# A second home for one 2 MB weight load, and fp32 token gathers of which two move into the first expert

## The chip, the cores and the metric

One Trainium2 chip, one core of it. The metric is device time of one execution in microseconds (us). Engines: TensorE (PE) multiplies, VectorE (DVE) and ScalarE (ACT) do elementwise work, GpSimd (POOL) here only splits weights, and SyncE (SP) issues nearly all loads from memory.

## What is computed

Two transformer blocks on 256 tokens of 1024 features, all in fp32. The first has attention and retention heads, then a mixture of 32 experts of which each token takes four, then a gated side product. The second has attention, a state-space branch and a dense FFN. What matters here is the mixture:

```python
logits = (xt @ w_router + b_router).astype(jnp.float32)
top_vals, top_idx = lax.top_k(logits, TOP_K)
gates = jax.nn.softmax(top_vals, axis=-1)
...
def expert_block(args):
    xb, e = args
    hgu = xb @ w_up_gate[e] + b_up_gate[e]
    x_glu = jnp.minimum(hgu[:, :D_EXPERT], SWIGLU_LIMIT)
    x_lin = jnp.clip(hgu[:, D_EXPERT:], -SWIGLU_LIMIT, SWIGLU_LIMIT)
    hact = x_glu * jax.nn.sigmoid(SWIGLU_ALPHA * x_glu) * (x_lin + 1.0)
    return hact @ w_down[e] + b_down[e]
...
return jnp.zeros((t, d), xt.dtype).at[slot_tok].add(ys * slot_gate[:, None].astype(xt.dtype))
```

`w_up_gate[e]` is 1024 x 2048 and `w_down[e]` 1024 x 1024 in fp32: 12 MB for each expert, 384 MB in all.

## The kernel before, in words

Everything lives in two tensors on the chip. `ring` has 12 slots of 128 x 2048 fp32 (1 MB each); `arena` holds activations and scratch, and its areas are reused from stage to stage. Outside the experts a weight piece lands in one of slots 0 to 7, ScalarE writes its rounded copy (`w_high`, type fp32r) into one of slots 8 to 11 (L1272), GpSimd replaces the piece by the rest (`w_low`, L2311), and TensorE makes three fp32r products of the parts (`product`, L524 to L526).

The experts use the weights unsplit, in fp32. One expert is six loads of 2 MB, each into two neighbouring slots: four of up weights (`UPS = 4`) and two of down weights, at slots `EXPERT_SLOT = (4, 6, 8, 10, 0, 2)`. TensorE counts the semaphore `w_used` up by one for each weight piece or expert load that it has finished with; SP waits for that count before it overwrites a home. SP's program is in order: the split pieces, then `first_expert(j)` in the order `FIRST_EXPERT = (0, 1, 2, 4, 3, 5)`, the first two of them early, then `expert_loads(e, e)` for experts 1 to 31 (L447 to L473). `before_experts` is 20, the number of split pieces ahead of the experts. Behind the experts come the next stage's pieces, first four of `w_ple_gate`.

Each expert computes at most 64 tokens (`CAP`). Tokens are gathered for a group of four experts at once: a **gather round** (`gather_round(q)`, L852) multiplies the token matrix (128 x 128 stationary pieces) by a one-hot matrix `OH4` of 256 columns (4 experts x 64 places) for two of the eight feature chunks. The tokens are the normalised state in two fp32r parts, `XNH` and `XNL`: ScalarE writes the high part (L1399), VectorE the rest (`token_low`, L1867). So a round is 2 chunks x 2 token blocks x 2 parts = 8 matmuls. VectorE scales each round's result from PSUM into the group's token buffer (`group_round_out`, L1930), `XG[0]` or `XG[1]` in turn.

Ahead of the loop TensorE makes all four rounds for the first group, into PSUM banks 6, 4, 5, 7, with three bias matmuls (L921) behind the first. The loop (L926) is written out for eight experts. For one expert: bias matmuls (`up_bias`, L873) with the selector `SEL` that VectorE prepares (L1926, L1927, semaphore `sel`), 8 chunks x 4 up matmuls (L883), the scatter of the expert before (L908), the spread of the gate matrix (L867), transposes of the hidden values (L890), 16 down matmuls (L901), and one gather round for the next group (L852). `q` is the expert's place in its group of four. A plain fp32 matmul stands in the trace as two records of one instruction each; an fp32r matmul as one.

Between the router and the loop VectorE's order is `token_low(0)`, top four, mask, `token_low(1)`, gates, slot numbers (L1901 to L1904), one-hot matrices (L1920), the four round results with `select(0)` behind the second, the overflow flags, and two multiplications that write the whole normalised state into `XN` in fp32 (L1951), which only a pass for experts with over 64 tokens reads.

## Time and profile before

| what | us |
|---|---|
| three runs | 1588.88, 1590.39, 1590.72 |
| median | 1590.39 |
| span of the profiled execution, first to last instruction | 1586.7 |
| TensorE busy | 1465.7 (92% of the span) |
| VectorE, ScalarE, GpSimd busy | 477.8, 412.1, 459.6 |
| bytes moved | 502.30 MB, 317 GB/s over the span |
| experts' up matmuls (L883), busy | 460.2 |
| experts' down matmuls (L901), busy | 235.3 |

The profiled execution's own device time is not listed apart from its span; the span lies 2.2 to 4.0 us below the three runs. A busy share is an average over stages with different limits: the experts' stage takes from about 175 to 1106 us of the span, and the split products fill the rest. The granted TensorE clock is 0.988 of full speed in the mean.

### The profile page before, as it was taken

The page shows a single profiled execution, that of the slowest core. Times are in us where ns is not written, and L with a number is a line of the kernel's source. Part 1 is how long each engine was busy: PE and PEld are TensorE (multiplying, and loading weights), DVE is VectorE, ACT ScalarE, POOL GpSimd, SP SyncE. Part 2 cuts the span into 40 slices and gives each one's busy share as a digit, 9 for nine tenths or more (in the row PEclk, how much of TensorE's full clock was granted, in tenths as well). Part 3 has the DMA queues.
Part 4 walks back from the last instruction along what each step waited for, and adds up shares of the span by engine and source line. Part 5 has one row for each costly group of instructions (what it writes and reads, how often), then busy time and mean ns, then how long its engine had stood idle before and what let it go on. Part 6 is the DMA issues. An engine that isn't in the chain of part 4 may idle for free.

```text
span 1586.7 us, 18714 instructions
## 1 busy us (share of the span) xinstructions
PE 1465.7 (92%) x7556; PEld 832.7 (52%) x7557; DVE 477.8 (30%) x844; ACT 412.1 (26%) x521; POOL 459.6 (29%) x356
## 2 busy tenths in 40 slices
PE   8999999998898889999888999899899999999998
PEld 7877533333333333333333333333698776799986
DVE  6536411111111111111111111112467586333211
ACT  6354301001001011010010010011754834453332
POOL 6836000000000000000000000001687763779994
PEclk9999999999999999999999999999999999999999
DMA  9533899999999999999999999999564332545540
GB/s 346 200 118 97 364 428 428 428 428 427 426 428 428 427 427 427 427 427 427 428 428 427 427 427 429 427 428 400 164 211 162 107 106 79 194 152 186 186 159 27
DMA packets 91174, 502.30 MB, mean 317 GB/s; under 512 B 7836, under 2 KB 38164, under 8 KB 66388
## 3 DMA queue, kind: packets, MB, share of 16 engines
q1 hardware_dynamic: 89600, 498.71, 77.6%
q10 hardware_dynamic: 1491, 2.36, 0.5%
q8 instruction: 68, 1.11, 0.3%
q14 instruction: 15, 0.12, 0.0%
HBM read 500.00 MB, written 1.05 MB: 316 GB/s over the span
## 4 chain that ended last, share of the span: by engine, by line
PE 54%; DMA 34%; DVE 5%; ACT 3%; issue 2%; POOL 2%; SPq 0%; DVEq 0%; ACTq 0%
DMA ring<-in_w_up_gate 32%; PE PS L883 15%; PE PS L524 9%; PE PS L526 9%; PE PS L525 9%; PE PS L901 5%; POOL w_low L2311 2%; DMA ring<-in_w_ple_gate 1%; PE PS L852 1%; PE PS L1148 1%; ACT w_high L1272 1%; PE PS L890 1%; DVE arena L1969 0%; DVE arena L1966 0%; DVE arena L1964 0%
## 5 line engine op out<-in xcount | busy, mean ns | idle before, releaser
L2311 POOL TENSOR_TENSOR w_low<-ring,w_high 128x512 fp32r<-128x512 f32 (+1 forms) x352 | 459.4, 1341 | 1105.9 <-ACT w_high L1272 1105.4
L883 PE MATMUL PS<-ring,arena 128*64 128x512 f32 x2048 | 460.2, 602 | 31.0 <-DMA ring<-in_w_up_gate 31.0
L883 PEld LDWEIGHTS PS<-ring,arena 128*64 128x64 f32 x2048 | 142.9, 138 | 332.1 <-issue 272.4
L901 PE MATMUL PS<-ring,arena 128*64 128x512 f32 x1024 | 235.3, 614 | 28.2 <-ACT arena L1428 28.2
L1419 ACT ACTIVATE arena<-arena 128x512 f32<-128x512 f32 x32 | 20.1, 630 | 765.8 <-DVE arena L1963 765.8
L1272 ACT ACTIVATE w_high<-ring 128x2048 fp32r<-128x2048 f32 (+1 forms) x89 | 166.5, 1881 | 124.0 <-PE PS L526 101.0
L1963 DVE TENSOR_SCALAR arena<-PS 128x512 f32<-128x512 f32 x32 | 22.1, 691 | 466.6 <-PE PS L883 466.6
L901 PEld LDWEIGHTS PS<-ring,arena 128*64 128x64 f32 x1024 | 75.2, 140 | 166.2 <-issue 166.2
L524 PE MATMUL PS<-w_high,XNT_h 128*128 128x512 f32 (+1 forms) x336 | 135.5, 403 | 5.9 <-DVE XNT_l L1676 4.6
L524 PE MATMUL PS<-XNT_h,w_high 128*128 128x256 f32 (+1 forms) x464 | 130.8, 282 | 2.2 <-DVE XNT_l L1659 1.3
L526 PE MATMUL PS<-w_high,XNT_l 128*128 128x512 f32 (+1 forms) x336 | 131.5, 391 | 0.0
L525 PE MATMUL PS<-w_low,XNT_h 128*128 128x512 f32 (+1 forms) x336 | 131.4, 391 | 0.0
L525 PE MATMUL PS<-XNT_l,w_high 128*128 128x256 f32 (+1 forms) x464 | 130.3, 281 | 0.0
L526 PE MATMUL PS<-XNT_h,w_low 128*128 128x256 f32 (+1 forms) x464 | 130.3, 281 | 0.0
L1972 DVE COPY arena<-PS 128x512 f32<-128x512 f32 x32 | 22.1, 691 | 282.6 <-PE PS L901 282.6
L524 PEld LDWEIGHTS PS<-XNT_h,w_high 128*128 128x128 f32 (+1 forms) x464 | 86.1, 186 | 3.5 <-issue 1.8
L525 PEld LDWEIGHTS PS<-XNT_l,w_high 128*128 128x128 f32 (+1 forms) x464 | 86.2, 186 | 0.2
L526 PEld LDWEIGHTS PS<-XNT_h,w_low 128*128 128x128 f32 (+1 forms) x464 | 86.2, 186 | 0.1
L524 PEld LDWEIGHTS PS<-w_high,XNT_h 128*128 128x128 f32 x336 | 63.5, 189 | 24.1 <-issue 8.4
L525 PEld LDWEIGHTS PS<-w_low,XNT_h 128*128 128x128 f32 x336 | 63.6, 189 | 14.3 <-issue 1.0
L526 PEld LDWEIGHTS PS<-w_high,XNT_l 128*128 128x128 f32 x336 | 63.3, 188 | 14.7
L908 PE MATMUL PS<-arena 64*128 64x512 f32 x256 | 63.6, 615 | 0.0
(369 smaller groups left out, 1429.1 us busy)
## 6 DMA issues: line engine op xcount, KB each, us to landing
ring<-in_w_up_gate SPq DMA_DIRECT2D x128, 2048.0 KB, 23.8
ring<-in_w_down SPq DMA_DIRECT2D x64, 2048.0 KB, 22.2
ring<-in_w_in SPq DMA_DIRECT2D x35, 1024.0 KB, 5.3
ring<-in_w_gate_up SPq DMA_DIRECT2D x22, 1024.0 KB, 5.1
ring<-in_w_down SPq DMA_DIRECT2D x11, 1024.0 KB, 4.7
ring<-in_w_out SPq DMA_DIRECT2D x8, 1024.0 KB, 4.9
ring<-in_w_ple_gate SPq DMA_DIRECT2D x4, 1024.0 KB, 22.2
ring<-in_w_ssd_proj SPq DMA_DIRECT2D x4, 1024.0 KB, 4.9
```

The lines of the kernel that those rows point to most:

```text
L524: nc.tensor.matmul(out, lhs[0], rhs[0], start=start, stop=False)
L525: nc.tensor.matmul(out, lhs[0], rhs[1], start=False, stop=False)
L526: return nc.tensor.matmul(out, lhs[1], rhs[0], start=False, stop=stop)
L852: ins = nc.tensor.matmul(PS[:, bank, (c % 2) * 256:(c % 2) * 256 + 256], part[:, tb * D + c * P:tb * D + (c + 1) * P], OH4[:, tb * 256:(tb ...
L883: ins = nc.tensor.matmul(PS[64 * (n % 2):64 * (n % 2) + 64, 4 + n // 2, :], x, w[:, n * 512:(n + 1) * 512], start=False, stop=c == KC - 1, ...
L901: ins = nc.tensor.matmul(PS[64 * n:64 * n + 64, 7, :], lhs, w[:, k, n * 512:(n + 1) * 512], start=(j, k) == (0, 0), stop=(j, k) == (1, 3))
L908: ins = nc.tensor.matmul(PS[:, 2 * tb + n, :], SPT[64 * n:64 * n + 64, tb * P:(tb + 1) * P], YS[64 * n:64 * n + 64, :], start=False, stop= ...
L1272: nc.scalar.activation(HIGH[m % BUF][:, 0:size(key)], slot(raw_slot(key))[:, 0:size(key)], ACT.Copy).then_inc(sem("w_high"), 1)
L1419: nc.scalar.activation(SIG, GLU, ACT.Sigmoid, scale=1.702).then_inc(sem(sig_out), 1)
L1963: ts(GLU, PS[:, 4, :], 7.0, None, ALU.min).then_inc(sem("glu"), 1)
L1972: V.tensor_copy(YS, PS[:, 7, :]).then_inc(sem("y_slots"), 1)
L2311: ins = nc.gpsimd.tensor_tensor(LOW[raw_slot(key)][:, at], slot(raw_slot(key))[:, at], HIGH[m % BUF][:, at].bitcast(F32), ALU.subtract)
```

## The change

It does five things.

1. The gathers read the normalised state in plain fp32. ScalarE's activation (the former L1399) writes it straight into `XN`, in the order of features that the experts' loads have. `XNH`, `XNL`, `token_low` and VectorE's two multiplications go. A round is now 2 chunks x 2 token blocks = 4 fp32 matmuls, with `OH4` in fp32.
2. The 2 MB of the arena that held `XNH` and `XNL` become `ODD_UP`, the home of the first up load of each odd expert, with a semaphore of its own, `landed_odd`. Even experts keep slots 4 and 5.
3. Expert 1's first up load is issued as soon as the last `w_out` piece is used, behind two of expert 0's. For later experts `first_up` waits for the use of the first up load two experts back.
4. Only rounds 0 and 1 of the first group are made ahead of the loop (banks 6 and 7). Rounds 2 and 3 of each group are made inside its first expert, in front of its third and fifth up chunk. Rounds 0 and 1 of the next group are made behind the second and third expert of a group; the first and fourth have none behind them.
5. VectorE builds the next group's one-hot matrices in the group's second expert instead of its first.

The core of the diff:

```diff
-        XNH, XNL = pair("XNS", 8192, 10240, 2048)
+        ODD_UP = area(8192, 4096)
-        OH4 = parts_at("OH4", arena_byte + 4 * 18688, 2 * GROUP * CAP)
+        OH4 = area(18688, 2 * GROUP * CAP)
-        FIRST_ROUNDS = (6, 4, 5, 7)
+        FIRST_ROUNDS = (6, 7)
...
-                sp.dma_start(slots2(EXPERT_SLOT[j]), src).then_inc(landed[EXPERT_SLOT[j]], 16)
+                if odd and j == 0:
+                    sp.dma_start(ODD_UP, src).then_inc(landed_odd, 16)
+                else:
+                    sp.dma_start(slots2(EXPERT_SLOT[j]), src).then_inc(landed[EXPERT_SLOT[j]], 16)
...
+            def first_up(e, odd):
+
+                sp.wait_ge(sem("w_used"), e * PER_EXPERT + (before_experts - 2 * PER_EXPERT + 1))
+                expert_load(e, 0, odd)
...
-            for j in FIRST_EXPERT[2:]:
+            for j in FIRST_EXPERT[2:4]:
                 first_expert(j)
-            with sp.Fori(1, E) as e:
-                expert_loads(e, e)
+            sp.wait_ge(sem("w_used"), place[("out", 1, 1)] + 1)
+            expert_load(1, 0, odd=True)
+            for j in FIRST_EXPERT[4:]:
+                first_expert(j)
+            with sp.Fori(0, E // 2 - 1) as i:
+                expert_loads(i * 2 + 1, i * 2 + 1, 1)
+                first_up(i * 2 + 2, odd=False)
+                expert_loads(i * 2 + 2, i * 2 + 2, 1)
+                first_up(i * 2 + 3, odd=True)
+            expert_loads(E - 1, E - 1, 1)
...
-                        for part in (XNH, XNL):
-                            ins = nc.tensor.matmul(PS[:, bank, (c % 2) * 256:(c % 2) * 256 + 256], part[:, tb * D + c * P:tb * D + (c + 1) * P],
-                                                   OH4[:, tb * 256:(tb + 1) * 256],
-                                                   start=(tb, part is XNH) == (0, True), stop=(tb, part is XNL) == (1, True))
+                        ins = nc.tensor.matmul(PS[:, bank, (c % 2) * 256:(c % 2) * 256 + 256], XN[:, tb * D + c * P:tb * D + (c + 1) * P],
+                                               OH4[:, tb * 256:(tb + 1) * 256], start=tb == 0, stop=tb == 1)
...
                     if q == 0:
-                        pe.wait_ge(sem("x_slots"), e + 3)
+                        pe.wait_ge(sem("x_slots"), e + 2)
                     up_bias()
                     for c in range(KC):
+                        if q == 0 and c == 2:
+                            gather_round(2)
+                        if q == 0 and c == 4:
+                            pe.wait_ge(sem("x_slots"), e + 3)
+                            gather_round(3)
                         if q == 0 and c == 6:
                             pe.wait_ge(sem("x_slots"), e + 4)
...
                     down(e)
-                    if q == 0:
+                    if q == 1:
                         pe.wait_ge(sem("onehot"), i * 2 + (u // GROUP + 2))
-                    gather_round(q)
+                    if q in (1, 2):
+                        gather_round(q - 1)
...
-                nc.scalar.activation(feature_pairs(XNH, tb), pairs_of(X, tb), ACT.Copy, scale=stat[:, 6 + tb:7 + tb]).then_inc(sem("xn_high"), 1)
+                nc.scalar.activation(feature_pairs(XN, tb), pairs_of(X, tb), ACT.Copy, scale=stat[:, 6 + tb:7 + tb]).then_inc(sem("tokens"), 1)
...
-            token_low(0)
...
-            token_low(1)
...
-            for tb in range(NTB):
-                link(ts(XN[:, tb * D:(tb + 1) * D], X[:, tb * D:(tb + 1) * D], stat[:, 6 + tb:7 + tb], None, ALU.mult))
```

The order of SP's instructions where the experts' loads begin, before: two loads of expert 0 (up, down), two more, then the loop over experts with the six loads of one each. The words in brackets are the semaphores that an instruction waits for.

```order
L448 DMA ring<-in_w_up_gate 128x4096 [waits w_used]
L448 DMA ring<-in_w_down 128x4096 [waits w_used]
L448 DMA ring<-in_w_up_gate 128x4096 [waits w_used]
L448 DMA ring<-in_w_down 128x4096 [waits w_used]
L472 UNCONDITIONAL_BRANCH
L472 ISA
L448 ISA [waits w_used]
L448 DMA ring<-in_w_up_gate 128x4096
```

The same place now:

```order
L456 DMA ring<-in_w_up_gate 128x4096 [waits w_used]
L456 DMA ring<-in_w_down 128x4096 [waits w_used]
L454 DMA arena<-in_w_up_gate 128x4096 [waits w_used]
L456 DMA ring<-in_w_up_gate 128x4096 [waits w_used]
L456 DMA ring<-in_w_down 128x4096 [waits w_used]
L489 UNCONDITIONAL_BRANCH
L489 ISA
L456 ISA [waits w_used]
L456 DMA ring<-in_w_up_gate 128x4096
```

Expert 1's first up load (to `arena`) now stands ahead of the last two loads of expert 0, and the loop begins with expert 1's second up load.

TensorE's order from the last gather matmuls ahead of the loop into expert 0, before (`OH_58` and `XNS` are `OH4` and the two token parts, `landed4` and `landed6` the arrival of the first two up loads):

```order
L852 MATMUL PS<-OH_58,XNS_h 128x256
L852 MATMUL PS<-OH_58,XNS_l 128x256
L925 UNCONDITIONAL_BRANCH [waits bias_low,late_in]
L925 ISA
L931 REGISTER_ALU [waits sel]
L873 MATMUL PS<-BUP,SEL 128x512 [waits x_slots]
L873 MATMUL PS<-BUP,SEL 128x512
L880 ISA
L883 MATMUL PS<-ring,arena 64x512 [waits landed4]
L883 MATMUL PS<-ring,arena 64x512 x7
L883 MATMUL PS<-ring,arena 64x512 [waits landed6]
```

The same place now:

```order
L945 UNCONDITIONAL_BRANCH [waits bias_low,late_in]
L945 ISA
L951 REGISTER_ALU [waits sel]
L891 MATMUL PS<-BUP,SEL 128x512 [waits x_slots]
L891 MATMUL PS<-BUP,SEL 128x512
L964 ISA
L903 MATMUL PS<-ring,arena 64x512 [waits landed4]
L903 MATMUL PS<-ring,arena 64x512 x7
L872 MATMUL PS<-arena 128x256 x4
L897 ISA
L903 MATMUL PS<-ring,arena 64x512 [waits landed6]
```

Round 2 (L872, four matmuls) has moved from ahead of the loop to between the first and the second up load of expert 0; round 3 stands likewise between the second and the third.

## Rows read from the trace of the kernel before

**Rows 1.** The page, part 2: GB/s in 40 equal slices of the span

```profile
GB/s 346 200 118 97 364 428 428 428 428 427 426 428 428 427 427 427 427 427 427 428 428 427 427 427 429 427 428 400 164 211 162 107 106 79 194 152 186 186 159 27
```

**Rows 2.** Windows, TensorE: length, busy time (instructions), granted clock, DMA share, GB/s

```profile
260.00:600.00 340.00, 306.69 (x1402) 0.98 1.01 428
```

**Rows 3.** The page, part 5: the experts' up matmuls

```profile
L883 PE MATMUL PS<-ring,arena 128*64 128x512 f32 x2048 | 460.2, 602 | 31.0 <-DMA ring<-in_w_up_gate 31.0
```

**Rows 4.** The chain of waits, end of the experts: start, us, what

```profile
1081.46 21.25 DMA ring<-in_w_ple_gate
...
1102.80 1.92 ACT w_high L1272
...
1104.79 19.98 POOL w_low L2311 x16
```

**Rows 5.** Timeline of SP's DMA issues: start, us, what, how many

```profile
154.06 0.34 SPq L448 DMA_DIRECT2D ring<-in_w_up_gate  x1
...
165.52 0.33 SPq L448 DMA_DIRECT2D ring<-in_w_up_gate  x1
...
179.72 0.35 SPq L448 DMA_DIRECT2D ring<-in_w_up_gate  x1
183.14 3.77 SPq L448 DMA_DIRECT2D ring<-in_w_up_gate  x2
...
198.21 3.77 SPq L448 DMA_DIRECT2D ring<-in_w_down  x2
206.85 3.77 SPq L448 DMA_DIRECT2D ring<-in_w_up_gate  x2
```

**Rows 6.** Windows of 2 us around the start of the experts

```profile
170.00:172.00 2.00, 2.00 (x8) 0.50 0.97 418
...
178.00:180.00 2.00, 2.00 (x12) 1.00 0.03 8
180.00:182.00 2.00, 2.00 (x12) 1.00 0.67 147
182.00:184.00 2.00, 2.00 (x12) 1.00 0.90 385
```

**Rows 7.** Timeline of VectorE ahead of the experts: start, us, what, [idle before <-releaser]

```profile
165.27 1.40 DVE L1867 SCALAR_TENSOR_TENSOR XNS_l<-arena,stat,XNS_h 128x512 fp32r<-128x512 f32 x2
...
167.44 0.22 DVE L1901 SCALAR_TENSOR_TENSOR slot_of<-PS,arena 128x64 f32<-128x64 f32 x1
...
173.45 0.69 DVE L1930 TENSOR_TENSOR arena<-PS,stat 128x512 f32<-128x512 f32 x1 [2.10 <-PE PS L852]
...
174.25 0.19 DVE L1927 CAST SEL<-cst 64x64 fp32r<-64x64 f32 x1
```

**Rows 8.** Timeline of TensorE ahead of the experts

```profile
166.39 0.39 PE L838 MATMUL PS<-arena,cst 128*128 128x32 f32 x2
...
167.58 0.64 PE L843 MATMUL PS<-cst,gate_of 128*32 128x128 f32 x8 [0.49 <-DVE gate_of L1898]
169.04 0.36 PE L852 MATMUL PS<-OH,XNS_h 128*128 128x256 f32 x1 [0.83 <-DVE OH L1920]
...
170.42 1.48 PE L921 MATMUL PS<-BUP,SEL 128*128 128x512 f32 x3
...
175.21 0.73 PE L873 MATMUL PS<-BUP,SEL 128*128 128x512 f32 x2
```

**Rows 9.** Timeline of TensorE: a gather round, and fp32 matmuls of 128x256

```profile
201.40 0.39 PE L852 MATMUL PS<-OH,XNS_h 128*128 128x256 f32 x1
...
202.46 0.63 PE L873 MATMUL PS<-BUP,SEL 128*128 128x512 f32 x2
...
1261.99 1.89 PE L1129 MATMUL PS<-arena 128*128 128x256 f32 x8
1263.72 1.02 PE L1138 MATMUL PS<-arena,cst 128*128 128x512 f32 x2
```

73 lines of the change are left out of this document (42 added, 31 removed).

## Prediction

> **What bounds the kernel now.** I read the page's slices first: from the sixth slice to the twenty-sixth the memory queues move 426 to 429 GB/s without a break [rows 1], and the windows show their share at 1.01 [rows 2]. That is the experts' loop: 192 transfers of 2048 KB, six for each of 32 experts (four of up weights, two of down weights). I call each a pair, since it fills two slots of the ring, and number them 1 to 192 in the order in which TensorE uses them. At 427 GB/s a pair of 2.097 MB takes 4.91 us. TensorE is idle before the up matmuls for 31.0 us in all because pairs are missing [rows 3], and the chain that ended last runs through the loop on DMA, leaves it over the first ple_gate piece, which comes behind pair 192 in the same queue, and goes on over the splits on GpSimd [rows 4]. So inside the loop nothing on TensorE, VectorE or ScalarE counts as long as the queue stays full. What counts is when the queue becomes full for good, and how much is left to move at that time.
>
> SP's issues show how it fills [rows 5]. Pairs 3 and 5 go out at 154.06 (two 2 MB loads one behind the other), pairs 4 and 6 at 165.52, and then all six pair homes are taken. Pair 7 waits until expert 0 has used pair 1: 179.72. Between, the queue is dry: 8 GB/s in 178 to 180, 147 and 385 in the next two windows [rows 6]. Those two hold 1.06 MB, which is 2.5 us at 427 GB/s, so full flow began at 181.5, 1.8 us after the issue. From there the queue is never dry: pair 11 would need 181.5 + 4 x 4.91 = 201.1, and the use of pair 5 that frees its home came at 198.21, with 1.8 us for the start 200.0. That margin of 1.1 us is small, and the prediction turns on it.
>
> **The change, part by part.**
>
> *The second home.* Pair 7 (the first of expert 1) is issued at 154.06 behind pairs 3 and 5. Five pairs then run from 155.8 to 155.8 + 5 x 4.91 = 180.4, with no gap. This fills the two dry stretches, moves 4.91 us of work ahead of the loop, and lets the queue wait for pair 2 instead of pair 1. Pairs 4 and 6 land some 5 us later than before; expert 0 needs pair 4 at about 190, so this costs nothing.
>
> *The order of work until expert 0.* The two `token_low` pieces go. The one of 1.40 us at 165.27 lay in front of the gates [rows 7]; without it VectorE waits for the position matmuls instead, which end at 166.39 + 0.39 = 166.78 [rows 8], not moved since TensorE comes to them from the side product. VectorE's slot arithmetic began at 167.44, so it gains 0.6 us, and the first gather round starts at 168.46 instead of 169.04. The two XN multiplications after the flags go too; nobody waited for them.
>
> *The price of a round.* A gather round was 8 fp32r matmuls, 1.06 us from 201.40 to 202.46 [rows 9]. It becomes 4 fp32 matmuls of 128x256, which stand in the trace as 8 records. The nearest rows are the 8 such records at 1261.99, followed at 1263.72 by the next line: 1.73 us, at full clock and behind full-width matmuls [rows 9]. The old round began with a first record 0.1 us longer, so bounds are 1.73 and 1.95; I take 1.85.
>
> *Start of expert 0.* Before, rounds 2 and 3 covered VectorE's copy and the selector; now TensorE waits for `sel`: 0.69 us for the copy and 0.99 us from the copy's start to the selector's end [rows 7]. With the clock at 2.4 GHz: 168.46 + 1.75 + 0.7 (three bias matmuls) + 1.75 = 172.7, drained at 172.8, plus 1.05 = 173.85 against 175.21 [rows 8]: 1.35 us earlier. But before, the granted clock was 0.50 from 170 to 172 [rows 6], that is 1.2 GHz, and the round from 169.04 to 170.42 and the three bias matmuls, 1.48 us with their drain, felt it. TensorE had been idle for 0.49 and 0.83 us and had run small matmuls before it fell. Now the first of these gaps goes and a new one of 1.05 us comes in front of expert 0. If the clock falls all the same, be it there or a little later, it costs 1.7 us, and expert 0 is 0.35 us later than before. Call the shift S: -1.35 to +0.35. One row with a fall after more idling does not decide it; I take the middle, -0.5.
>
> *Expert 0.* Two rounds of 1.85 us lie inside its up matmuls, in front of pairs 2 and 3. Nothing hides them: expert 0's pairs have landed, TensorE is never idle there. VectorE's copy of round 2 (0.69 us) is hidden by pair 2's 3.43 us. Now the queue: pair 8 can go at 183.14 + 1.85 + S, flowing at 186.8 + S. Pair 9 follows at 192.1 + S (it was issued at 186.58, the last 0.33 us of the 3.77 from 183.14), pair 10 behind it. Pair 11 needs expert 0's first down pair used: 198.21 + 3.7 + 1.8 + S = 203.7 + S. Pairs 8 to 10 are through at 201.9 + S or sooner, so the queue goes dry once more and **pair 11 sets the end**. Pair 12 has 1.5 us of margin (issued at 201.65 before; 201.65 + 3.7 + 1.8 = 207.1 against 208.6), pair 13 has a free home, and pair 14 is at 214.7 against 218.4, because expert 0 no longer ends with a round. From there on the queue is full.
>
> *Sum.* Before, pair 11 flowed at 201.1; now at 203.7 + S. All that comes behind it is the same in bytes and order, and the chain leaves the loop over the first ple_gate piece. So the end moves by 2.6 + S: +1.25 to +2.95, and with 1.73 or 1.95 for a round +1.0 to +3.2; I take **+2.1 us**. The extra home gives 4.9 us of work ahead; waiting for pair 2 and then for the down pair, behind two added rounds, takes it back and a little more.
>
> By the Trainium skill (DMA: Bandwidth & Descriptors, section "Anatomy of one DMA") a transfer costs about 2.0 us plus its bytes at 436 GB/s, which would be 4.8 us a pair. The rows say 427 GB/s and 1.8 us; with the page's figures pair 11 would have flowed at 200.9 before and 203.9 + S now, a loss 0.4 us greater.
>
> *What costs nothing.* The steady rounds: per expert 0.79 us more on TensorE, covered by the queue (29.5 us for six pairs against 27.13 us from 179.72 to 206.85 [rows 5]). The last round, which expert 31 no longer makes: 1.06 us off TensorE, but the chain behind the loop is held by ple_gate's landing at 1102.7 and 19.98 us of GpSimd splits [rows 4]. ple_gate issued earlier: it stands behind pair 192 as before.
>
> **The rivals.**
>
> *A. TensorE becomes the bound (slower).* 31 experts with 0.79 us more are 24.5 us, and TensorE's idle time on missing pairs is 31.0 us [rows 3]. That leaves 6.5 us. Against: fewer waits should mean fewer falls of the clock, each of which costs about 1.7 us. For: falls in the last experts come too late to be made up. It decides from about four falls more than before; with two beyond that the price is 3.4 us, so 1590.4 + 2.1 + 3.4 = 1596. Beside it: the Trainium skill (TensorE: Matmul & The Clock Gate, "HAM oscillation") has TensorE throttled when it idles for data again and again, so fewer waits would help it, and this rival would be less likely. Chance 0.13.
>
> *B. Only pair 8 binds.* If the stretch from expert 0's last up matmul to its down pair were shorter than 198.21 shows, or rounds cost no more than the old ones, the end moves by 186.8 + S - (181.5 + 4.91) = +0.4 + S, 1590.3 with the middle S. Against: the down stretch isn't touched. Chance 0.09.
>
> *C. The queue itself gets faster (faster).* With seven homes more loads are in the queue. The share is 1.01 and the mean 428 GB/s [rows 2], with slices up to 429 [rows 1]. If the mean rose by 0.7%, the 186 pairs behind pair 6 (913 us) would shrink by 6.4, giving 1590.4 + 2.1 - 6.4 = 1586. Against: the share shows no empty time to win. Chance 0.06.
>
> **How the numbers follow.** The sum stands against the profiled execution, whose span is 1586.7 us; its own time isn't listed apart, but the three runs (1588.88 to 1590.72) lie 2.2 to 4.0 us above the span, and the change touches nothing outside. I set it on the median: 1590.39 + 2.1 = **1592.5 us**. Forecast 0.72, A 0.13, B 0.09, C 0.06. A measurement of this kernel can tell about 0.2% (3.2 us) from no change. Of the forecast's 0.72 some 0.14 lie above +3.2 us, since two clock falls or the dear round are enough: slower 0.27, faster 0.06 (C), same 0.67. The range leaves out C and the far half of A: with the runs' own 0.9 us it is 1588.4 to 1596.5.
>
> **What would show it.** In the trace of the changed kernel: SP issues an up load to the arena right behind the two at 154; the next one only at about 184.5; expert 0's first down pair is used at about 201.4; GB/s drops between 202 and 203.5, a dip that is absent now; no dip from there on; TensorE's idle time on missing pairs falls from 31 to some 10 us; the first ple_gate split begins about 2 us after 1102.80. I am wrong if the queue is full from pair 8 on (B), if TensorE no longer waits for pairs in the last experts (A), or if expert 0 starts outside 173.8 to 175.6.

## The result and the profile after

| | before | changed |
|---|---|---|
| median of 20 runs, us | 1589.83 | 1592.22 |
| lowest to highest | 1587.31 to 1592.10 | 1590.17 to 1594.19 |
| span of the profiled execution | 1586.7 | 1588.8 (its own time 1590.65) |
| TensorE busy | 1465.7 | 1480.2 |
| TensorE idle for missing pairs, up matmuls | 31.0 | 19.6 |

The ratio is 1.0015, with a 95% interval of 1.0009 to 1.0021: 2.4 us more, by more than its noise and by less than 0.2%. The forecast was 2.1 us more. Two figures of the profiled execution are not typical of the changed kernel: it is the second shortest of the twenty, and its mean granted clock, 0.997, is the highest of them (0.987 to 0.997, median 0.990). The kernel before has a median clock of 0.989 over all its executions on record, and 0.988 in the profiled one.

The timeline of SP in the changed kernel (start, length, engine and line, what was issued) answers to [rows 5]:

```profile
155.15 0.43 SPq L454 DMA_DIRECT2D arena<-in_w_up_gate  x1
...
184.07 0.35 SPq L456 DMA_DIRECT2D ring<-in_w_up_gate  x1
201.20 0.33 SPq L456 DMA_DIRECT2D ring<-in_w_down  x1
...
205.25 0.33 SPq L456 DMA_DIRECT2D ring<-in_w_up_gate  x1
```

Pair 7 goes out at 155.15 into the arena. Pair 8 follows at 184.07, 29 us later, and pair 11 at 201.20, against 198.21 before. Pair 13 (205.25) finds a free home. The changed kernel's windows (stretch, its length, TensorE's busy time with the number of its instructions, granted clock, DMA share, GB/s) answer to [rows 6]; the last two, long ones serve further down:

```profile
170.00:172.00 2.00, 2.00 (x11) 1.00 0.96 410
...
180.00:182.00 2.00, 2.00 (x12) 1.00 0.23 98
182.00:184.00 2.00, 2.00 (x11) 1.00 0.03 8
184.00:186.00 2.00, 2.00 (x10) 1.00 0.65 131
...
200.00:202.00 2.00, 2.00 (x12) 1.00 0.52 221
202.00:204.00 2.00, 2.00 (x12) 1.00 0.97 238
204.00:206.00 2.00, 2.00 (x12) 1.00 0.98 418
...
140.00:226.00 86.00, 79.96 (x388) 1.00 0.80 325
260.00:600.00 340.00, 314.70 (x1419) 1.00 1.01 428
```

The first dry spot, from 177 to 181.5 before, now comes later, from 180.5 to 186; a second one, at 201 to 203, is new. From 204 on the queue is full for good, as it was from 181.5 before. The timelines of the changed kernel around the start of expert 0, TensorE's first and then VectorE's, answer to [rows 7] to [rows 9]:

```profile
168.50 1.97 PE L872 MATMUL PS<-arena 128*128 128x256 f32 x8 [0.76 <-DVE arena L1947]
...
174.05 0.73 PE L891 MATMUL PS<-BUP,SEL 128*128 128x512 f32 x2 [1.16 <-DVE SEL L1954]
...
178.29 1.99 PE L872 MATMUL PS<-arena 128*128 128x256 f32 x8
180.22 2.37 PE L903 MATMUL PS<-ring,arena 128*64 128x512 f32 x10
```

VectorE's:

```profile
173.72 0.19 DVE L1954 CAST SEL<-cst 64x64 fp32r<-64x64 f32 x1
```

Expert 0 starts at 174.05 (175.21 before), held by the selector for 1.16 us, and the round inside it takes 1.93 us. The end of the experts on the changed kernel's chain of waits answers to [rows 4]:

```profile
1079.31 25.46 DMA ring<-in_w_ple_gate
...
1104.85 1.92 ACT w_high L1309
```

The first split of a ple_gate piece begins at 1104.85, which is 2.05 us later than before, and the span is 2.1 us longer. The whole loss of the profiled pair stands here already.

### The profile page after: what moved, and what is told of

Same layout as the page of the kernel before. It is cut to its first block, busy times and chain, and to the rows that moved or that the text cites. A ratio compares the mean times of both kernels' runs of the same rounds, so it can differ in the third digit from the quotient of the medians.

```text
span 1588.8 us, 18631 instructions
## 1 busy us (share of the span) xinstructions
PE 1480.2 (93%) x7540; PEld 844.1 (53%) x7541; DVE 473.3 (30%) x836; ACT 412.2 (26%) x521; POOL 459.0 (29%) x356
## 4 chain that ended last, share of the span: by engine, by line
PE 63%; DMA 24%; DVE 5%; ACT 3%; issue 2%; POOL 2%; SPq 0%; DVEq 0%; ACTq 0%
DMA ring<-in_w_up_gate 22%; PE PS L903 18%; PE PS L545 10%; PE PS L547 9%; PE PS L546 9%; PE PS L921 8%; PE PS L872 3%; POOL w_low L2340 2%; DMA ring<-in_w_ple_gate 2%; PE PS L910 1%; PE PS L1185 1%; DVE arena L1994 1%; DVE arena L1997 1%; DVE arena L1992 1%; PE PS L891 1%
## 5 line engine op out<-in xcount | busy, mean ns | idle before, releaser
L903 PE MATMUL PS<-ring,arena 128*64 128x512 f32 x1792 | 400.8, 597 | 19.6 <-DMA ring<-in_w_up_gate 19.6
L903 PEld LDWEIGHTS PS<-ring,arena 128*64 128x64 f32 x1792 | 123.9, 137 | 276.8 <-issue 231.4
L921 PE MATMUL PS<-ring,arena 128*64 128x512 f32 x1024 | 228.5, 599 | 28.5 <-ACT arena L1465 28.5
L921 PEld LDWEIGHTS PS<-ring,arena 128*64 128x64 f32 x1024 | 73.5, 137 | 161.5 <-issue 161.5
L872 PE MATMUL PS<-arena 128*128 128x256 f32 x272 | 67.7, 392 | 0.8 <-DVE arena L1947 0.8
```

Of the source, the lines that this page charges most:

```text
L872: ins = nc.tensor.matmul(PS[:, bank, (c % 2) * 256:(c % 2) * 256 + 256], XN[:, tb * D + c * P:tb * D + (c + 1) * P], OH4[:, tb * 256:(tb + ...
L903: ins = nc.tensor.matmul(PS[64 * (n % 2):64 * (n % 2) + 64, 4 + n // 2, :], x, w[:, n * 512:(n + 1) * 512], start=False, stop=c == KC - 1, ...
L921: ins = nc.tensor.matmul(PS[64 * n:64 * n + 64, 7, :], lhs, w[:, k, n * 512:(n + 1) * 512], start=(j, k) == (0, 0), stop=(j, k) == (1, 3))
```

## The experiments

These readings of each profiled execution serve below. The first is what the queue had moved by 226 us, from the window 140 to 226. In the kernel before that window reads:

```profile
140.00:226.00 86.00, 80.49 (x405) 0.98 0.82 334
```

334 GB/s over 86 us are 28.7 MB; the changed kernel has 325 (its row is above). The difference is 0.77 MB, at 427 GB/s 1.8 us of flow; this is what "late" means in the table, a minus sign being early. The second is the start of the first ple_gate split, the third the start of TensorE's last scatter behind expert 31. "Split to end" is the span less the first split; the clocks are those of the windows 1100 to 1130 and 1130 to 1160; "chain" says whether the chain of waits leaves the loop over ple_gate's load and GpSimd's splits or over TensorE's last down matmuls and scatter.

| kernel | pair 8 / 11 issued | GB/s (late, us) | first split | last scatter | span | split to end | clock 1100 to 1130 / to 1160 | chain | median | ratio (95%) |
|---|---|---|---|---|---|---|---|---|---|---|
| before | 183.14 / 198.21 | 334 (0) | 1102.80 | 1106.66 | 1586.7 | 483.9 | 1.00/1.00 | load |  |  |
| changed | 184.07 / 201.20 | 325 (1.8) | 1104.85 | 1108.09 | 1588.8 | 483.9 | 1.00/1.00 | load | 1592.22 | 1.0015 (1.0009, 1.0021) |
| e1, no second home | 184.17 / 201.31 | 324 (2.0) | 1105.34 | 1108.97 | 1590.8 | 485.5 | 1.00/0.94 | load | 1592.28 | 1.0018 (1.0006, 1.0030) |
| e2, four rounds ahead | 183.96 / 199.01 | 330 (0.8) | 1104.47 | 1109.09 | 1591.3 | 486.8 | 1.00/0.94 | TensorE | 1592.68 | 1.0019 (1.0010, 1.0029) |
| e3, fp32 alone | 183.86 / 198.93 | 331 (0.6) | 1103.70 | 1108.37 | 1589.3 | 485.6 | 1.00/1.00 | TensorE | 1591.55 | 1.0013 (1.0004, 1.0022) |
| e4, inner rounds twice | 185.71 / 206.25 | 300 (6.8) | 1111.02 | 1118.47 | 1599.4 | 488.4 | 1.00/1.00 | TensorE | 1597.90 | 1.0046 (1.0028, 1.0063) |
| e5, cheap rounds | 181.78 / 197.65 | 338 (-0.8) | 1102.88 | 1107.66 | 1588.4 | 485.5 | 0.94/1.00 | TensorE | 1590.06 | 0.9999 (0.9989, 1.0008) |
| e6, moved rounds alone | 182.40 / 200.47 | 328 (1.2) | 1103.82 | 1109.11 | 1588.6 | 484.8 | 0.95/1.00 | TensorE | 1591.66 | 1.0013 (1.0004, 1.0022) |
| e7, home for a down load | 183.91 / ahead | 329 (1.0) | 1104.83 | 1108.42 | 1590.3 | 485.5 | 1.00/0.94 | load | 1592.09 | 1.0015 (1.0006, 1.0024) |
| e8, e7 with four rounds ahead | 183.73 / ahead | 338 (-0.8) | 1102.10 | 1106.76 | 1587.9 | 485.8 | 1.00/0.94 | TensorE | 1591.42 | 1.0011 (1.0002, 1.0020) |
| e8 again | 183.88 / ahead | 338 (-0.8) | 1102.35 | 1108.69 | 1589.5 | 487.2 | 0.97/0.94 | TensorE | 1591.38 | 1.0009 (1.0000, 1.0018) |
| e9, one idle round | 182.01 / 197.30 | 340 (-1.2) | 1102.03 | 1105.93 | 1587.6 | 485.6 | 1.00/0.94 | load | 1589.78 | 1.0007 (0.9997, 1.0017) |
| e10, split tokens, e7's home | 182.50 / ahead | 349 (-3.0) | 1100.38 | 1103.88 | 1584.6 | 484.2 | 1.00/1.00 | TensorE | 1590.70 | 1.0007 (0.9995, 1.0020) |
| e10 again | 184.05 / ahead | 341 (-1.4) | 1101.84 | 1105.71 | 1590.4 | 488.6 | 0.89/0.94 | TensorE | 1590.44 | 1.0008 (0.9996, 1.0019) |

The kernel before had medians of 1589.2 to 1589.5 beside these. Each median of the experiments is of 11 or 12 runs (e4: 6) and good to about 1.5 us, so differences of 1 us between them prove nothing; the rows of the traces are sharper.

Two things can be read off the table at once. Behind the loop two paths end close together: the load's and TensorE's. Where the chain is the load's and the clock stays at 1.00, the end comes 483.9 us behind the first split (before, changed); with one fall of the clock between 1130 and 1160 it comes at 485.5 or 485.6 (e1, e7, e9), so that fall costs 1.6 us. And where the queue was made earlier than in the changed kernel, the chain went over to TensorE in all kernels but e7 and e9, so that the split's lead is not worth its full size.

The lateness in bytes and that of the first split are not the same thing. From 226 to 1080 us no kernel but e4 gains or loses more than 0.3 us of bytes against the kernel before, and yet in these kernels the first split is between 0.2 us less and 1.0 us more late than the bytes at 226 say (e7: 1.0 by bytes, 2.03 by the split; e2: 0.8 and 1.67; e5: -0.8 and +0.08). Part of that is in the landings. A load counts as landed when the last of its sixteen signals has come, and the trace has them in two groups of eight that drift apart in the loop: in the kernel before 1.35 us at 223, 5.4 us for the first ple_gate piece (the eighth signal at 1097.30, the last at 1102.72). In the changed kernel it is 1.09 us at 224 and 7.1 us at the end (1097.65 and 1104.77). So against the kernel before the early half came 0.35 us later there and the late half 2.05. What makes the halves drift, and differently in different kernels, is open; a first split is good to about 1 us as a measure of how late the queue is.

### e1_one_home: the changed kernel without its second home

```diff
-            sp.wait_ge(sem("w_used"), place[("out", 1, 1)] + 1)
-            expert_load(1, 0, odd=True)
...
+            with sp.Fori(1, E) as e:
+                expert_loads(e, e)
```

> The changed kernel without the second home: all first up loads go to slots 4 and 5 again, pair 7 waits for the use of pair 1; gathers stay fp32 and two rounds stay inside expert 0. Theory (pair 11, behind two rounds, sets the end): pair 7 flows at about 180.4, pairs 8 to 10 behind it, so pair 11 still waits for expert 0's first down pair (issue about 201.2) and the time is that of the changed kernel, 1592.2 within 0.8 us; the second home is worth nothing here. Rival (the second home carries its 4.9 us of work ahead and something else eats more): 1597, with the first ple_gate piece landing near 1109 instead of 1104.8.

Measured: 1592.28, the time of the changed kernel. (Its profiled span is 2.0 us longer than the changed kernel's: 0.5 at the first split, 1.6 the fall of the clock behind it.) SP's timeline, with the issues of pairs 7, 8 and 11:

```profile
178.68 0.35 SPq L456 DMA_DIRECT2D ring<-in_w_up_gate  x1
184.17 0.34 SPq L456 DMA_DIRECT2D ring<-in_w_up_gate  x1
...
201.31 0.33 SPq L456 DMA_DIRECT2D ring<-in_w_down  x1
```

Pair 7 now goes at 178.68 instead of 155.15, and pairs 8 and 11 where they went with the home, within 0.11 us. By 226 us the queue has moved the same within one in the last digit (324 and 325). The 4.9 us of work loaded ahead are worth nothing, since pair 11 is late either way. This is the prediction's central step, shown by taking the home away.

### e2_four_ahead: all four rounds ahead of the loop, the rest as changed

```diff
-            for q in range(2):
-                if q == 1:
+            for q in range(4):
+                if q == 3:
                     pe.wait_ge(sem("gT"), 1)
...
-                        if q == 0 and c == 2:
-                            gather_round(2)
...
-                    if q in (1, 2):
-                        gather_round(q - 1)
+                    gather_round(q)
```

> The changed kernel with all four fp32 rounds ahead of the loop and one round behind every expert, as before; second home and fp32 gathers stay. Theory: expert 0 starts about 1.0 us later than in the kernel before (176.2 against 175.21; up to 1.7 us later still if the clock falls), nothing is added inside it, pair 11 is issued at about 199.2 and the queue dips only a few tenths there: 1590.3, 1.9 us less than the changed kernel (0.2 us less if the clock falls). Rival (it is the fp32 rounds as such, 0.8 us more on TensorE per expert, that cost time): as slow as the changed kernel, 1592.2.

Measured: 1592.68, a miss; the number is the rival's. Pair 11 was issued at 199.01 as expected, but the time did not fall, and the trace shows the reason for a part of it. By the rule of the prediction (1.8 us from issue to flow) pair 10 was through at 183.96 + 1.8 + 3 x 4.91 = 200.5, and a gap of a few tenths was left. The windows of e2 say otherwise:

```profile
200.00:202.00 2.00, 2.00 (x12) 1.00 0.63 246
202.00:204.00 2.00, 2.00 (x11) 1.00 1.18 401
204.00:206.00 2.00, 2.00 (x11) 1.00 0.80 328
206.00:208.00 2.00, 2.00 (x12) 1.00 0.97 401
```

From 200 to 208 some 0.66 MB are missing against 427 GB/s, 1.6 us, though pair 11 went out 1.5 us before pair 10 was through. The queue was 0.8 us late by 226 and the first split 1.7 us. From there to the end it took 486.8 us and not 483.9: the chain runs over TensorE, with a fall of the clock between 1130 and 1160 on it, and over a fp32 round of 1.92 us behind expert 31, which the changed kernel does not make. In that place the rival holds. So part of the expected gain was lost to a dip that I had priced at nothing, and part behind the loop.

### e3_fp32_alone: the kernel before with fp32 gathers only

One home as in e1, and all four rounds ahead as in e2; against the kernel before this leaves the tokens' form:

```diff
-                        for part in (XNH, XNL):
-                            ins = nc.tensor.matmul(..., part[:, tb * D + c * P:tb * D + (c + 1) * P],
+                        ins = nc.tensor.matmul(..., XN[:, tb * D + c * P:tb * D + (c + 1) * P],
...
-            token_low(0)
...
-            token_low(1)
```

> The kernel before with fp32 gathers alone: four rounds ahead, one behind every expert, no second home. Theory: expert 0 starts 1.0 us later than before without a fall of the clock (2.7 with one), pair 7 waits for pair 1 and flows at about 182.5, and the end moves by the same 1.0 us: 1590.9. Rival (fp32 rounds in the loop bind): 1592 or more, with fewer dry spots in the queue at the start.

Measured: 1591.55, pair 7 issued at 180.44 (0.72 us later than before), the first split 0.9 us later. The theory's mechanism and about its size are there at the split; 1.7 us more came behind it, on TensorE's path with no fall of the clock (last scatter 1.7 us later than before). The interval of the time (0.6 to 3.5 us) holds both. Against e1 it lacks only the move of the two rounds; against the changed kernel it lacks the home as well.

### e4_rounds_twice: the two inner rounds made twice

```diff
                         if q == 0 and c == 2:
+                            gather_only(2)
                             gather_round(2)
                         if q == 0 and c == 4:
                             pe.wait_ge(sem("x_slots"), e + 3)
+                            gather_only(3)
                             gather_round(3)
```

`gather_only` makes the same four matmuls into the same bank without the signal.

> The changed kernel with the two rounds in a group's first expert made twice, each into the same PSUM bank; the result is the same. 8 groups make 16 more rounds of 1.73 to 1.93 us, of which two lie in expert 0. Theory (only expert 0's uses count, the queue hides the rest): the two in expert 0 move pair 11 by 3.6 us: 1595.8, and the queue's dip ahead of pair 11 grows by as much. Rival A (TensorE has no reserve left in the loop): the 14 later ones, 26 us, exceed the 19.6 us that TensorE still waits for pairs, and the time rises by 10 us or more; the waits for pairs vanish in the last experts.

Measured: 1597.90, 5.7 us over the changed kernel where 3.6 were expected (6 runs, and the profiled one, 1601.27, is the slowest of them). Pair 11 went at 206.25, 5.05 us later: 3.6 us of it the two rounds, 1.4 a fall of the clock behind 200 (0.71 in the window 202 to 206). The view of waits over the loop has in e4 two rows above 10 us, TensorE's waits for ScalarE and for VectorE inside an expert, and both stand in the changed kernel too. The longest (line, what it waited for: us in total, times, longest one):

```profile
PE PS L928 <- ACT arena L1474: 28.0, 32, 0.9
```

The same view of the changed kernel, the row that has no counterpart there:

```profile
PE PS L903 <- DMA ring<-in_w_up_gate: 19.6, 19, 1.2
```

The wait for pairs, 19.6 us in the changed kernel, is gone, and the last scatter begins 7.45 us behind the first split instead of 3.24.

So both theories hold in part: the start gives 5.0 us. With 26 us more in the later groups the queue has gaps inside the loop as well (399 GB/s from 556 to 564, 352 from 678 to 684; 2 us of flow between 500 and 700), and TensorE has become the bound at the end (the last scatter is 10.4 us later than in the changed kernel). Rival A of the prediction is real; the changed kernel stands 16 to 20 us of TensorE work away from it, going by what it and its siblings with the same rounds (e1: 16.9, e7: 16.2) still wait for pairs.

### e5_rounds_cheap: rounds of four fp32r matmuls

```diff
+        XNR = parts_at("XNR", arena_byte + 4 * 2048, 2048)
-        OH4 = area(18688, 2 * GROUP * CAP)
+        OH4 = parts_at("OH4", arena_byte + 4 * 18688, 2 * GROUP * CAP)
```

The low part of the tokens is left out of what the experts get.

> The changed kernel with the tokens in fp32r, high part only, and so rounds of 4 fp32r matmuls, about 0.5 us each instead of 1.75 to 1.93; the low part of the tokens is left out of the experts' input. Theory: expert 0 starts about 2.6 us earlier than in the changed kernel and has 2.8 us less inside, pair 11 is issued at about 195.8: 1586.8, 5.4 us less than the changed kernel, and the wait of pair 8 then nearly equals that of pair 11. Rival (the rounds' price doesn't matter, the second home's transfers disturb the start): within 1 us of the changed kernel.

Measured: 1590.06, 2.2 us less than the changed kernel, and no different from the kernel before. The direction and the cause are confirmed (the rounds' price decides), the size is less than half. Two steps of my sum failed. Expert 0 began at 173.02, 1.0 us earlier and not 2.6, because the clock fell during the first rounds. And pair 11 did not set the end alone. The windows of e5, and the issue of pair 9 from SP's timeline:

```profile
170.00:174.00 4.00, 2.83 (x11) 0.69 1.02 438
...
188.00:190.00 2.00, 2.00 (x10) 1.00 0.85 279
...
198.00:200.00 2.00, 2.00 (x12) 1.00 0.86 328
200.00:202.00 2.00, 2.00 (x12) 1.00 0.96 352
202.00:204.00 2.00, 2.00 (x12) 1.00 0.94 319
```

```profile
186.02 0.34 SPq L457 DMA_DIRECT2D ring<-in_w_up_gate  x1
```

Pair 9 went out at 186.02, 2.5 us before pair 8 could be through (183.6 + 4.9), and still the window at 188 has 279 GB/s, 0.7 us of flow lost. From 198 to 204 another 1.3 us is missing.

### e6_inside_alone: the kernel before with only the rounds moved

Split tokens and one home as before; the two rounds go inside:

```diff
-        FIRST_ROUNDS = (6, 4, 5, 7)
+        FIRST_ROUNDS = (6, 7)
...
                     for c in range(KC):
+                        if q == 0 and c == 2:
+                            gather_round(2)
+                        if q == 0 and c == 4:
+                            pe.wait_ge(sem("x_slots"), e + 3)
+                            gather_round(3)
```

> The kernel before with only the rounds moved: two fp32r rounds (8 matmuls, about 1.1 us) inside a group's first expert, two ahead; tokens stay split, one home. Theory: expert 0 starts 0.5 to 1.5 us earlier, has 2.2 us more inside; pair 11 is issued at about 199.6 and flows at 201.4 against 201.1: +0.3 us, 1590.1, no difference that can be measured. Rival (moving the rounds is itself what costs 2.4 us): 1592.2.

Measured: 1591.66, which fits the rival's number and not mine. The windows of e6 tell what came between, with the issue of pair 10 in SP's timeline behind them:

```profile
194.00:196.00 2.00, 1.13 (x5) 0.81 1.02 430
196.00:198.00 2.00, 2.00 (x6) 0.50 0.96 410
```

```profile
190.56 0.33 SPq L448 DMA_DIRECT2D ring<-in_w_up_gate  x1
```

The clock fell to 1.2 GHz (0.50) in expert 0's down stretch: pair 11 (200.47) came 9.91 us behind pair 10, against 8.20 us in the kernel before. That is 1.7 us. Expert 0 had begun at 173.18, and without the fall pair 11 would have gone at 198.76. So against the kernel before pair 11 is 0.55 us later by the rounds' place and 1.7 by a fall of the clock. The 0.55 is too small for the move: the profiled execution of the kernel before had a fall at its first rounds (0.50 from 170 to 172) and this one had none there. e9 below has the same start without a fall, with expert 0 at 174.08 instead of 175.21; against that the move costs 1.7 us at pair 11. Whether the fall belongs to the move or to this execution can't be said from one trace. What I had left out is that falls inside expert 0 count in full.

### e7_down_home and e8_down_home_four_ahead: the home for pair 11 instead of pair 7

```diff
-                if odd and j == 0:
+                if odd and j == UPS:
                     sp.dma_start(ODD_UP, src).then_inc(landed_odd, 16)
...
-            expert_load(1, 0, odd=True)
+            expert_load(1, UPS, odd=True)
```

The waits and the down matmuls follow. e8 has e2's order of rounds besides.

> The changed kernel with the second home given to the first down load of odd experts instead of the first up load: pair 11 is loaded ahead, pair 7 waits for pair 1 (flows at about 180.4), pair 12 waits for the use of pair 6. Theory: pair 11 no longer binds; pair 12, issued at about 204.6 and flowing at 206.4, does, which is 1.4 to 1.5 us better than the changed kernel: 1590.8. Rival (the end is set elsewhere than at expert 0's down pairs): 1592.2 as the changed kernel.

> The kernel with fp32 gathers, four rounds ahead, and the second home for the first down load of odd experts. Theory: expert 0 starts 1.0 us later than before, pair 7 flows at 182.5, pair 12 at 204.4, pair 13 (expert 2's first up load, behind expert 0's round) at about 210.5 binds: 1589.4, 0.4 us less than the kernel before and 2.8 less than the changed one; 1.7 us more if the clock falls at the first rounds. Rival (homes give nothing as long as expert 0's uses are what they are): equal to the fp32 kernel with four rounds ahead and one home.

SP's timeline in e7, pairs 7 and 12, and its windows:

```profile
178.40 0.33 SPq L456 DMA_DIRECT2D ring<-in_w_up_gate  x1
...
204.49 0.33 SPq L456 DMA_DIRECT2D ring<-in_w_down  x1
```

```profile
200.00:202.00 2.00, 2.00 (x12) 1.00 0.50 213
202.00:204.00 2.00, 2.00 (x12) 1.00 0.00 0
204.00:206.00 2.00, 2.00 (x12) 1.00 0.53 106
206.00:208.00 2.00, 2.00 (x12) 1.00 0.76 279
...
210.00:212.00 2.00, 2.00 (x12) 1.00 1.08 352
212.00:214.00 2.00, 2.00 (x12) 1.00 0.89 336
214.00:216.00 2.00, 2.00 (x12) 1.00 0.90 377
```

In e7 pair 7 flows without a gap and pair 12 (204.49) binds, both as the theory had it. By 226 us the queue is 0.8 us ahead of the changed kernel and not 1.4: pair 13 went out at 208.90, 2.3 us before pair 12 was through (206.3 + 4.9), and from 210 to 216 another 1.0 us of flow is missing. And of the 0.8 us nothing reaches the first split: it is where it was (1104.83) and the time too (1592.09), a miss. Of the first ple_gate piece's signals the eighth came 0.24 us earlier than in the changed kernel (1097.41), the last at the same time. (Split to end is 485.5, with the fall between 1130 and 1160.) In e8 the queue is 2.6 us ahead of the changed kernel by 226 and the first split 2.75 us earlier; the time came out at 1591.42, 2 us over what I expected. It is the rival's number: e3, with the same rounds and one home, took 1591.55. So I ran it once more:

> The kernel e8_down_home_four_ahead a second time, unchanged. Its trace had the first ple_gate split 0.7 us ahead of the kernel before, its time was 2.0 us longer. Theory of the falls (expert 0's start is late by 1.7 us where the clock falls at the first rounds, as in most executions, and the profiled one was without): again 1590.5 to 1591.5, and a profiled execution whose expert 0 uses pair 1 at about 182 rather than 180.3. Rival (the profiled execution is typical and the first time was off): 1589.4 or less.

1591.38 again. But the profiled execution used pair 1 at 180.45, not at 182: expert 0's start was not late, and my explanation by falls at the first rounds fell. The last scatter did differ between the two executions of the same kernel, 1106.76 and 1108.69, with first splits 0.25 us apart; their spans differ by 1.6. Both chains run over TensorE there, so what the last expert loses on TensorE counts in full: in these kernels the load is no longer what ends last, and both have a fall of the clock between 1130 and 1160 besides.

### e9_one_idle_round: a round more behind a group's first up matmuls, in the kernel before

```diff
+                    if q == 0:
+                        pe.wait_ge(sem("x_slots"), e + 4)
+                        pe.wait_ge(sem("onehot"), i * 2 + (u // GROUP + 2))
+                        gather_only(0)
```

`gather_only` here makes a round's eight matmuls on the split tokens once more, without the signal.

> The kernel before with one fp32r round more (8 matmuls into a bank that is overwritten later, 1.0 us; the result is the same) behind the up matmuls of a group's first expert, so that pair 11 is issued at 199.25 instead of 198.21. As the prediction's margin has it (1.8 us from issue to flow, pair 10 through at 201.1) pair 11 would flow at 201.05 and nothing would move. Rival, from the dips that runs with pair 11 issued one to two microseconds ahead of the queue's end showed: a load has to be issued about 3 us ahead of the end of the one in front, and 0.7 to 1.0 us is lost: the bytes moved by 226 us fall by 0.3 to 0.4 MB, and the time is 1590.3.

Inconclusive, for two reasons. The profiled execution had no fall of the clock at the first rounds, so expert 0 began 1.1 us earlier and pair 11 went at 197.30, before its time in the kernel before. And the round hardly moved pair 11. TensorE's timeline, the kernel before first, then e9:

```profile
192.76 0.75 PE L890 MATMUL PS<-cst,arena 128*128 128x128 f32 x4 [0.64 <-DVE arena L1969]
194.38 5.80 PE L901 MATMUL PS<-ring,arena 128*64 128x512 f32 x26 [0.87 <-ACT arena L1428]
```

```profile
174.08 0.73 PE L882 MATMUL PS<-BUP,SEL 128*128 128x512 f32 x2
...
191.96 0.65 PE L899 MATMUL PS<-cst,arena 128*128 128x128 f32 x4
193.48 5.80 PE L910 MATMUL PS<-ring,arena 128*64 128x512 f32 x26 [0.87 <-ACT arena L1441]
```

From expert 0's start to its down matmuls it is 19.17 us before (175.21 to 194.38) and 19.40 in e9: of the round's 1.1 us only 0.2 arrive, because it fills the 0.64 us for which TensorE waited for VectorE ahead of the transposes. So pair 11 still had a lead of 2.7 us (pair 10 through at 178.59 + 1.8 + 4 x 4.91 = 200.0), and the windows behind 200 show no dip (426 and 451 GB/s). The ratio (0.9997 to 1.0017) holds both expectations. What the run does show is a cheaper place for a round in expert 0: behind the up matmuls and not between them. No run has the changed kernel's rounds there.

### e10_split_down_home: the best that the readings suggest

Tokens split again, so that a round costs 1.0 us, and e8's order and home. The low part of the tokens lies in three pieces in free room. The kernel ran twice:

```diff
+        XNH = parts_at("XNS_h", arena_byte + 4 * 2048, 2048)
+        XNL0 = parts_at("XNS_l0", arena_byte + 4 * 12288, 1024)
+        XNL1 = [parts_at(f"XNS_l{1 + h}", arena_byte + 4 * at, 512) for h, at in enumerate((19200, 22016))]
```

> Tokens split in two fp32r parts as before (the low part in other free room of the arena, the high part where the fp32 state was), four rounds of 1.0 us ahead and one behind every expert, and the second home for the first down load of odd experts. Theory: expert 0 starts as before (175.2), pair 7 flows at 181.5, pair 11 is already there, pair 12 flows at 203.3 and pair 13, issued at 206.85 1.3 us ahead of the queue's end, at about 209.3: that is 1.6 us ahead of the kernel before. 1587.9, 0.1% faster than before, 4.3 us less than the changed kernel. Rival (a home ahead gives nothing, whatever stands in expert 0): 1589.5.

> The kernel e10_split_down_home a second time, unchanged: its profiled execution took 1586.47, the shortest of all so far, and its first ple_gate split began 2.4 us ahead of the kernel before, but its median was 1590.7 and its runs spread from 1586.5 to 1594.8. Theory (the queue's gain is real, the spread comes from behind and around it): the first ple_gate split again at 1100 to 1101.5, a median of 1588 to 1589.5. Rival (the profiled execution was a lucky one): first split at 1102 or later and a median above 1590.

The windows of the first execution:

```profile
170.00:172.00 2.00, 1.94 (x13) 1.00 1.00 426
...
1100.00:1130.00 30.00, 27.51 (x124) 1.00 0.60 204
1130.00:1160.00 30.00, 26.52 (x157) 1.00 0.70 219
```

The same windows of the second, and one of 5 us inside them:

```profile
170.00:172.00 2.00, 1.91 (x10) 0.73 1.07 459
...
1100.00:1130.00 30.00, 27.74 (x114) 0.89 0.65 220
1110.00:1115.00 5.00, 5.00 (x17) 0.50 0.82 272
1130.00:1160.00 30.00, 26.53 (x127) 0.94 0.52 159
```

The first profiled execution did what the theory says, and more (1.6 us ahead was expected; 0.5 of the rest is expert 0, which began at 174.71 without a fall of the clock): 3.0 us ahead by 226, the first split 2.4 us ahead, a span 2.1 us shorter than before, and no fall of the clock behind the loop. The second met a fall at 170 and used pair 1 1.56 us later (180.62 against 179.06); it was 1.0 us ahead at the split, and then lost 4.4 us to falls at 1110 (0.50 in the window 1110 to 1115) and after 1130: its span is 3.7 us longer than before. The medians, 1590.70 and 1590.44, are not below the kernel before (ratio 0.9995 to 1.0020), so the first execution is not the usual one; they lie over the rival's 1589.5. The queue's lead is in both traces, and by the medians about as much is lost again. That it is lost to falls of the clock behind the loop is shown by the second trace alone. No version here beats the kernel before.

## Why the prediction was right

**The result.** +2.1 us were forecast (+1.0 to +3.2 by its bounds), +2.4 measured. The class, no difference of 0.2%, is right too.

**What bounds.** Right. The queue is full from 204 to the end of the loop, and what it is late by at 226 (1.8 us) is close to what the first split (2.05) and the span (2.1) are late by. That the three agree to 0.3 us is partly luck: in e2, e5 and e7 the split is 0.9 to 1.0 us later than the queue's bytes say.

**Pair 11 sets the end.** Right, by e1: the same kernel without the home has the same issue of pair 11 and the same time.

**The price of a round.** 1.93 us from 178.29 to 180.22, inside the bounds (1.73 to 1.95); 1.85 was taken. Two of them, 3.86 us, are the largest term. What they cost pair 11 is a little more: from expert 0's start to the issue of pair 11 it was 23.00 us (175.21 to 198.21) and is 27.15 (174.05 to 201.20), 4.15 us for the two where 3.7 were put in.

**Expert 0's start.** S was -1.16 us in the profiled execution, close to the bound without a fall of the clock; the middle of -0.5 was taken. The clock was at 1.00 from 170 to 172, where it had been 0.50. Round 0 began at 168.50 (168.46 forecast), `sel` held TensorE for 1.16 us. Pair 11 was then issued at 201.20 (198.21 + 4.15 - 1.16), and 201.4 was forecast. The two errors (S taken 0.66 us too late, the rounds 0.45 us too cheap) nearly cancelled, and that is luck.

There is more luck in S. Nearly all of the 1.16 us is the fall of the clock that the profiled execution of the kernel before happened to have: e9, which has that kernel's start and no such fall, begins expert 0 at 174.08, and the changed kernel at 174.05. Set beside e9 the change does nothing for expert 0's start, and costs 3.0 us of flow by 226 (e9 at -1.2, changed at 1.8) and 2.8 us at the first split. The 2.1 us between the two profiled executions are good for that pair; how often either kernel has the fall is not known, and the medians' 2.4 us lie between.

**Dips.** A dip from 202 to 203.5 was forecast; it lies from 201 to 203. None afterwards: right.

**Mis-sized: TensorE's waits for pairs.** "Some 10 us" were forecast, 19.6 measured. The forecast time does not hang on it. The step is "31 experts with 0.79 us more are 24.5 us": the work did come (TensorE's busy time rose by 14.5 us), but the granted clock rose from 0.988 to 0.997 over the span, and from 0.98 to 1.00 in 260 to 600 (the last row of the windows above). Busy time there is 314.70 us against 306.69 [rows 2]. This execution was a quiet one, as the clocks of the other nineteen show. In e1 and e7, which have the same rounds and a clock of 0.992, the waits are 16.9 and 16.2 us.

Fewer waits are not what goes with a higher clock here. By the median clock of all executions on record the kernels with two fp32 rounds inside expert 0 have 0.990 (changed) and 0.992 (e1, e7, and e4, which waits for no pair at all). The kernels with the same fp32 rounds all behind the experts have 0.988 (e2, 18.2 us of waits) and 0.987 (e3, 16.2 us), and e8, with 13.7 us, has 0.988: no more than the kernel before with its 31.0 us (0.989). The Trainium skill (TensorE: Matmul & The Clock Gate, "HAM oscillation") has TensorE throttled when it waits for data again and again; the waits here, 1.3 us at the longest in the kernel before, made no difference that these clocks show. What sets a kernel's clock here is open.

**Rival A** was rightly held unlikely and rightly there: e4 shows TensorE as the bound at 26 us more. **Rival B** did not occur; the nearest to it is e5, where cheap rounds gave 2.2 of the 2.4 us back. **Rival C** had no sign: the flow in the loop is 427 and 428 GB/s in all kernels but e4, where TensorE holds it up (423 from 500 to 700).

**The price of a load.** The prediction set beside its own rows what the Trainium skill (DMA: Bandwidth & Descriptors, "Anatomy of one DMA") gives, about 2.0 us and 436 GB/s. The page fits these to transfers issued from GpSimd; the loads here are SyncE's. With pair 11's issue at 201.20 the rows' figures make it 1.9 us late, the page's 2.3; 1.8 was measured, nearer to the rows.

**Where the reasoning was thin.** The margin of 1.1 us at pair 11 was computed with 1.8 us from issue to flow. That figure comes from an empty queue. e2, e5 and e7 show that a load issued 1.5 to 2.5 us ahead of the end of the one in front still loses 0.7 to 1.6 us of flow; with 2.7 (e9) and 2.9 us (before) no loss is seen. In the changed kernel this hardly mattered, since pair 11 was late by more. And the prediction followed one path out of the loop, the load's. That was right for this change, which moves that path later (483.9 us from the split to the end in both kernels), but a second one, over TensorE's last expert, lies close behind: of e10's lead of 2.4 us at the split 2.1 reached the end, the most in any trace.

**Open.** The falls of the clock between 1100 and 1160 are in nine of the twelve experiments' traces and in neither of the two kernels'; in e10 one execution has them and the other not. Whether the changed kernel has them less often than the variants can't be said from one trace of each, and so it stays open how much of a variant's median they make.

## What to carry to other kernels

A buffer more lets a saturated queue run ahead only if the next buffer to come free is not later for it: look for the load whose home is released last against its turn in the queue, here the first down pair, and count everything between. Work that is free in the steady state, since the queue hides it, is paid in full in the first item of the loop, before the queue is saturated. To test what a buffer is worth, take it away and look whether the binding issue moves. Before work goes into that first item, look where its engine waits there anyway: e9's round, put in front of such a wait, cost 0.2 us where its length is 1.1.

## What the hardware showed that I had not expected

- A load that is issued shortly ahead of the end of the one before does not join without loss: 279 GB/s in the 2 us where 2.5 us of lead were there (e5), 352 and 336 where 2.3 were (e7), 246 and 328 where 1.5 were (e2), against 427. With 2.7 us (e9) and 2.9 us of lead (the kernel before, pair 11) no dip is to be seen.
- One and the same kernel uses its first pair 1.56 us apart in two executions, with one fall of the clock at its first gather rounds (e10), and the queue carries that shift over 920 us to the first split (1100.38 and 1101.84). A single fall behind the loop costs 1.6 us (e1, e7, e9): two thirds of what the whole change does.
- The sixteen landing signals of one load come in two groups of eight that drift apart in a full queue: 1.35 us at 223 and 5.4 at 1100 in the kernel before, 1.09 and 7.1 in the changed one, while the flow stays at 427 to 428 GB/s. The load is there when the late group is, so two kernels with the same bytes moved can start the next stage 1 us apart.
